# Expert matrices issued in another order, with longer pieces for each partition

## What is computed

```python
grp_logits = (t @ w_r1) + b_r1
grp_prob = jax.nn.softmax(grp_logits, axis=-1)
grp_idx = jnp.argmax(grp_logits, axis=-1)
fine_sel = fine_logits[token, grp_idx]                 # 8 experts of the group
top_val, top_idx = lax.top_k(fine_sel, 2)
gate = grp_gate * jax.nn.softmax(top_val, axis=-1)
exp_idx = grp_idx[:, None] * 8 + top_idx
...
def expert_block(args):
    xb, e = args
    a = jax.nn.silu(xb @ w1[e]) * (xb @ w3[e])         # w1, w3: 1024 x 512
    return a @ w2[e]                                   # w2: 512 x 1024
...
y = y.at[row_tok].add(yb * row_gate[:, None])
```

## Time and profile before

| | us |
|---|---|
| median of 3 runs (lowest, highest) | 3587.39 (3586.43, 3595.63) |
| the profiled execution | 3589.83 |
| its span, first to last instruction | 3588.1 |
| TensorE busy | 3068.5 (86%) |
| VectorE, ScalarE, POOL busy | 1046.3, 747.3, 164.6 |
| DMA traffic | 441.15 MB, of which 201 MB are expert matrices |

### The profile page before, as it was taken

One profiled execution on the slowest core, in us unless ns is written; L12 is line 12 of the kernel. 1 busy time (PEld: TensorE's weight loads), 2 busy tenths in 40 slices (PEclk: granted clock), 3 DMA queues, 4 the chain that ended last, 5 costly groups with the idle time before them and its releaser, 6 DMA issues. The chain is left out here.

```text
span 3588.1 us, 34649 instructions
## 1 busy us (share of the span) xinstructions
PE 3068.5 (86%) x13906; PEld 1847.5 (51%) x13906; DVE 1046.3 (29%) x2162; ACT 747.3 (21%) x1627; POOL 164.6 (5%) x265
## 2 busy tenths in 40 slices
PE   7999974877787588999898999899949774888998
PEld 3448633444444465666455564455523343364674
DVE  3440622000000201055210273333126575200242
ACT  2111810000000102243210383100003110112341
POOL 0000001111110000000000020011100001000000
PEclk9999996899889799999999999999969887999999
DMA  6663432999999311110011200022233414011200
GB/s 228 234 229 124 177 147 62 347 351 365 361 364 358 115 48 32 42 48 24 0 36 60 83 2 1 24 94 87 88 101 132 150 63 148 0 41 53 77 1 24
DMA packets 244208, 441.15 MB, mean 123 GB/s; under 512 B 31420, under 2 KB 111820, under 8 KB 240725
## 3 DMA queue, kind: packets, MB, share of 16 engines
q1 hardware_dynamic: 234278, 416.81, 33.2%
q0 software_dynamic: 9776, 22.18, 1.8%
HBM read 408.73 MB, written 37.81 MB: 124 GB/s over the span
## 5 line engine op out<-in xcount | busy, mean ns | idle before, releaser
L2002 PE MATMUL moe_ph<-expert_weights,moe_x_T 128*64 128x256 f32 x2048 | 275.6, 429 | 100.4 <-issue 99.0
L344 PE MATMUL hyena_in_main<-hT,weight_slots 128*128 128x256 f32 (+1 forms) x1024 | 330.5, 486 | 1.4 <-PEq L985 1.4
L2002 PEld LDWEIGHTS moe_ph<-expert_weights,moe_x_T 128*64 128x64 f32 x2048 | 172.4, 155 | 206.7 <-issue 155.0
L344 PEld LDWEIGHTS hyena_in_main<-hT,weight_slots 128*128 128x128 f32 x1024 | 194.5, 190 | 137.2 <-issue 124.0
L344 PE MATMUL swa_in_main<-hT,weight_slots 128*128 128x512 f32 (+1 forms) x576 | 189.4, 489 | 6.6 <-DMA weight_slots<-b_w_in 5.2
L344 PE MATMUL mla_down_main<-hT,weight_slots 128*128 128x512 f32 (+1 forms) x448 | 168.4, 538 | 19.8 <-DMA weight_slots<-a_w_in 19.8
L1403 PE MATMUL qkv_main<-hT,weight_slots 128*128 128x512 f32 (+1 forms) x384 | 167.8, 580 | 0.9 <-PEq L985 0.9
L1194 PE MATMUL post_y<-expert_weights,hT 128*128 128x512 f32 x384 | 165.1, 592 | 0.0
L344 PEld LDWEIGHTS swa_in_main<-hT,weight_slots 128*128 128x128 f32 x576 | 109.9, 191 | 86.4 <-issue 73.7
L344 PE MATMUL mla_up_main<-expert_weights,weight_slots 128*128 128x512 f32 (+1 forms) x416 | 146.4, 511 | 2.8 <-PEq L985 2.4
L344 PEld LDWEIGHTS mla_down_main<-hT,weight_slots 128*128 128x128 f32 x448 | 88.0, 198 | 100.2 <-issue 75.0
(11 more groups left out here) (357 smaller groups left out, 4117.9 us busy)
## 6 DMA issues: line engine op xcount, KB each, us to landing
expert_weights<-w SPq DMA_DIRECT2D x96, 2048.0 KB, 15.2
first_w_out<-w_mod SPq DMA_DIRECT2D x12, 2048.0 KB
expert_weights<-w_mod SPq DMA_DIRECT2D x12, 2048.0 KB, 8.0
weight_slots<-w_in SPq DMA_DIRECT2D x16, 1024.0 KB
weight_slots<-c_w_in SPq DMA_DIRECT2D x16, 1024.0 KB
weight_slots<-a_w_in SPq DMA_DIRECT2D x14, 1024.0 KB
scr_spectra<-expert_weights SPq DMA_DIRECT2D x12, 1024.0 KB, 3.8
expert_weights<-scr_spectra SPq DMA_DIRECT2D x12, 1024.0 KB, 4.9
```

The lines of the kernel that those rows point to most:

```text
L344: mm = pe.matmul(main[u][0:unit.rows, 0:unit.cols], lhsT, rhs, start=(c == 0), stop=(c == r.kc - 1))
L2002: mm = pe.matmul(bank[half * T:(half + 1) * T, 0:HF], x_T[:, c, :], w[:, c, half * HF:(half + 1) * HF], start=(c == 0), stop=(c == KD - 1))
```

## The change

Two things change.

*Order.* SP's loop now follows the order in which TensorE frees the slots: in step b it waits for the first up product of b and issues W1 of b + 2, waits for the second up product of b and issues W3 of b + 2, then waits for the down product of b - 1 and issues W2 of b + 1. W1 and W3 have a semaphore each, and TensorE waits for W3 only before the second up product.

*Layout.* W1 and W3 are laid out "(p c) n": partition p gets rows 8p to 8p + 7, one contiguous piece of 16 KB. W2 is "(h p j) n": partition p gets rows 2p and 2p + 1 of each half, two pieces of 8 KB. Contraction chunk c now holds the features 8p + c, so the pieces of x that are turned take every 8th column, and the transposes of the activations every 2nd.

```diff
@@ ExpertWeights.__init__
-        self.w1, self.w3, self.w2 = (a[k][0].rearrange("e (c p) n -> e p c n", p=P) for k in ("w1", "w3", "w2"))
+        self.flat1, self.flat3 = flat[0:2], flat[2:4]
+        self.flat2 = [t.rearrange("p (h m) -> p h m", h=2) for t in flat[4:6]]
+        self.w1, self.w3 = (a[k][0].rearrange("e (p c) n -> e p (c n)", p=P) for k in ("w1", "w3"))
+        self.w2 = a["w2"][0].rearrange("e (h p j) n -> e p h (j n)", h=2, p=P)
...
+    def load_gate(self, sp, e):
+
+        sp.dma_start(self.flat1[e % 2], self.w1[e]).then_inc(Stage.w1_in[e % 2], 16)
+
     def load_up(self, sp, e):
 
-        s = e % 2
-        sp.dma_start(self.W1[s], self.w1[e]).then_inc(Stage.w13_in[s], 16)
-        sp.dma_start(self.W3[s], self.w3[e]).then_inc(Stage.w13_in[s], 16)
+        sp.dma_start(self.flat3[e % 2], self.w3[e]).then_inc(Stage.w3_in[e % 2], 16)
 
     def load_down(self, sp, e):
 
-        sp.dma_start(self.W2[e % 2], self.w2[e]).then_inc(Stage.w2_in[e % 2], 16)
+        sp.dma_start(self.flat2[e % 2], self.w2[e]).then_inc(Stage.w2_in[e % 2], 16)
@@ turn_rows
-        mm = pe.matmul(px[:, c * T:(c + 1) * T], x[:, c * P:(c + 1) * P], consts["identity"][0:T, 0:T],
+        mm = pe.matmul(px[:, c * T:(c + 1) * T], x[:, c:D - KD + c + 1:KD], consts["identity"][0:T, 0:T],
@@ turn_act_rows
-        mm = pe.transpose(pa[:, c * P:(c + 1) * P], act_rows[:, c * P:(c + 1) * P], consts["identity"][:])
+        mm = pe.transpose(pa[:, c * P:(c + 1) * P], act_rows[:, c:FF // 2 - 1 + c:2], consts["identity"][:])
@@ experts_stage, SP
-                for b in range(experts.EARLY, E):
-
-                    sp.wait_ge(s_h3, b - 1)
-                    experts.load_up(sp, b)
-                    sp.wait_ge(s_py, b - 1)
-                    experts.load_down(sp, b)
+                for b in range(E):
+
+                    if b + 2 < E:
+                        sp.wait_ge(s_h1, b + 1)
+                        experts.load_gate(sp, b + 2)
+                        sp.wait_ge(s_h3, b + 1)
+                        experts.load_up(sp, b + 2)
+                    if experts.EARLY <= b + 1 < E:
+                        sp.wait_ge(s_py, b)
+                        experts.load_down(sp, b + 1)
@@ experts_stage, TensorE
-                    pe.wait_ge(Stage.w13_in[b % 2], (b // 2 + 1) * 32)
+                    pe.wait_ge(Stage.w1_in[b % 2], (b // 2 + 1) * 16)
                     pe.wait_ge(s_silu, b)
                     up_product(pe, ph1, x_T[b % 2], experts.W1[b % 2]).then_inc(s_h1, 1)
                     if b:
                         turn_act(b - 1)
+                    pe.wait_ge(Stage.w3_in[b % 2], (b // 2 + 1) * 16)
                     pe.wait_ge(s_act, b)
```

More of the change, by code:

```diff
@@ L67 @@
 class Stage:
-    POOLS = ((99, 167), (167, 235))
+    POOLS = ((99, 166), (166, 233))
     turn = 0
@@ L84, in begin @@
         Stage.weights_in = [nc.alloc_semaphore(name=f"weights_in{k}", num=239 + k) for k in range(2)]
-        Stage.w13_in = [nc.alloc_semaphore(name=f"expert_w1_w3_in{k}", num=235 + k) for k in range(2)]
+        Stage.w1_in = [nc.alloc_semaphore(name=f"expert_w1_in{k}", num=233 + k) for k in range(2)]
+        Stage.w3_in = [nc.alloc_semaphore(name=f"expert_w3_in{k}", num=235 + k) for k in range(2)]
         Stage.w2_in = [nc.alloc_semaphore(name=f"expert_w2_in{k}", num=237 + k) for k in range(2)]
@@ L1154, in _ @@
                     for e in range(experts.EARLY):
+                        experts.load_gate(sp, e)
                         experts.load_up(sp, e)
@@ L2252, in step @@
                         sp.wait_ge(s_h3[s], k)
-                        for dst, src in ((W1, experts.w1), (W3, experts.w3)):
-                            sp.dma_start(dst[s], src[ds(e, 1)].rearrange("o p c n -> (o p) c n"))\
+                        for dst, src in ((experts.flat1, experts.w1), (experts.flat3, experts.w3)):
+                            sp.dma_start(dst[s], src[ds(e, 1)].rearrange("o p m -> (o p) m"))\
                                 .then_inc(s_w13[s], 16)
                         sp.wait_ge(s_py[s], k)
-                        sp.dma_start(W2[s], experts.w2[ds(e, 1)].rearrange("o p c n -> (o p) c n")).then_inc(s_w2[s], 16)
+                        sp.dma_start(experts.flat2[s], experts.w2[ds(e, 1)].rearrange("o p h m -> (o p) h m"))\
+                            .then_inc(s_w2[s], 16)
                     over_blocks(sp, step)
```

## The result

The changed kernel takes 3699.3 us (median of 4 runs, 3698.3 to 3700.0), the kernel before in the same comparison 3589.7: a ratio of 1.030, 95% interval 1.028 to 1.032. That is 110 us slower. The forecast was 58 us slower, 3645 us, with a range that ended at 3685; the time lies outside it. The profiled execution has a span of 3698.3 us.

A forecast was written before the change was run, and what follows sets the result against it. The gather loop was to bound every step of the changed kernel: 15.1 + 1.9 (stride) + 2.6 (longer pieces) + 0.6 (clock) = 20.2 us against 18.18, over 29 steps +58 us, 3645 us. Range 3548 to 3685.

The forecast's parts named there:

- The gather loop becomes the bound of all steps: Expert stage: the loop of down product, gather, turning, down product grows from 15.1 to 20.2 us, above the transfers' 15.9.
- The gather among longer pieces, +2.6 us: DMA queues: the gather's small packets take turns with longer weight pieces, so it lands 2.6 us later per step.
- Five and four: Of some 9 weight pieces between an engine's gather and scatter packets, five were taken as 8 KB and four as 16 KB.
- the rival with the engine turning inside a piece: DMA engines switch queues within a piece, so the gather isn't slower: loop 17.0 us, 3553 us; chance 0.22.
- Strided turning, +1.9 us: TensorE's turning of tokens: 16 loads of every 8th column at 235 instead of 116 ns, +1.9 us per expert.
- The rival of a free step of 8: Turning with every 8th column costs nothing extra: loop 17.7 us, -14 us, 3573 us; chance 0.12.
- the prediction's note on lines of 16 bytes: SBUF reads, citing the skill: a step of 8 floats pays, a step of 2 floats does not.
- The clock, +0.6 us: TensorE's clock falls after idling for the gather: between 0 and 2.9 us per step, taken as 0.6.
- First and last step about cancel: Ends of the stage: first loads go out some 4 us earlier, three more turnings on the path cost 5.7.
- The order, up to 0.8 us: SP's load queue no longer runs dry when the down product is late; can return up to 0.8 us per step.
- the 17.4 of the sum from the earlier trace: DMA time per expert in small pieces: W1 and W3 11.4 us, W2 5.3, gather and scatter 0.7.
- Neither cost comes, 15.9 to 16.3 us a step, 3527: Rival: gather not slower and stride free, so transfers bound the stage; -60 us, 3527 us; chance 0.06.

The follow-up runs named there:

- gathers ahead: Changed kernel with POOL issuing each gather four blocks ahead and in front of the scatter: 3542.5 us, ratio 0.986 to the kernel before.
- both comparisons of pieces: Changed kernel with 4 KB pieces (3648.5 us) against the changed kernel; new layout in old order (3709.9) against kernel before with strided turning (3642.7).
- order alone: New order of the loads with the old layout, against the kernel before: 3556.5 us, ratio 0.990.
- gathers ahead in the old layout: Old layout (pieces of 2 and 4 KB) in the new order, with gathers issued four blocks ahead: 3545.2 us, ratio 0.988 to the kernel before.
- gathers ahead and the rows stored in another order: Changed kernel with gathers four blocks ahead and token rows stored so that the turning loads contiguous columns: 3524.5 us, ratio 0.982 to the kernel before.

## Why the prediction was wrong

- **The gather loop becomes the bound of all steps: right.** The issues of W2 lie 20.4 to 23.9 us apart in 28 of 29 steps, where 19.4 and 15.1 alternated, the DMA share is 0.77 (0.8 was named), each turning waits for its gather, and gathers ahead take the loss away.
- **The gather among longer pieces, +2.6 us: right.** 6.7 + 2.6 = 9.3 was the landing expected, 9.3 is the median; both comparisons of pieces give 2.3 and 2.4. How it comes about shows in the queues between 871 and 877 and between 876 and 878, the answer to the earlier trace rows:

```profile
q1 hardware_dynamic: 176, 1.97, 85.9%
q0 software_dynamic: 151, 0.38, 16.6%
...
q1 hardware_dynamic: 55, 0.90, 106.1%
q0 software_dynamic: 33, 0.00, 0.9%
```

  Scatter and gather are 160 packets, as before, and 151 of them go in the 6 us in which the weights' queue moves 176: 112 of 8 KB until 874 and 64 of 16 KB behind it, 7 and 4 for each engine. Five and four had been put in; the 11 pieces of this step make 7 x 0.154 + 4 x 0.463 = 2.9 us by the same prices, so that 2.6 fits so closely is in part luck. In the last 2 us the weights' 55 packets are of 16 KB each and the gather's 33 are tiny, and yet both queues are served. A piece of 16 KB held an engine for 1.061 x 32 / 55 = 617 ns there; 629 had been worked out. (The Trainium skill, "DMA: Bandwidth & Descriptors", SWDGE vs HWDGE vs iDMA, says that the engine goes round robin between its queues and that a packet, the unit of the turns, is preferably 4096 bytes or less. The trace agrees with the turns; the packets here are 16 KB, so the rival with the engine turning inside a piece fell.)
- **Strided turning, +1.9 us: right in size,** 4.0 us against 1.9, +2.1. The rival of a free step of 8 fell. The step of 2 floats is small but not the nothing that the prediction's note on lines of 16 bytes makes of it: the two transposes of the activations take 0.50 us instead of 0.44, their weight loads 207 ns each instead of 142.
- **The clock, +0.6 us: here the prediction failed.** The steps of 21.93 leave 21.93 - 2.8 - 9.3 - 4.0 = 5.8 us for the down product, 2.1 more than the 3.7 of before. The 1.5 us too few make 1.5 x 29 = 44 us, and with 0.2 per step of the turning nearly all of the 52 that were missing. The step of reasoning that failed is "most waits of 1 to 2 us cost nothing, so I take 0.6". It was read off the kernel before, where few turnings wait at all, and "order alone" shows that it does not carry over: with contiguous columns and waits of 1.4 to 2.0 us, 8 down products of 13 took 5.2 us or more. It was not asked what the strided turning does to the clock by itself (5.35 us in 23 of 29 steps, with no wait); nor was a wait of over 4 us priced as the one of 3.00 us in the earlier trace rows, which cost 2.9, though the same paragraph had worked out such a wait for every step. The upper bound of 2.9 was written down and then left out of the range: 15.1 + 1.9 + 2.6 + 2.9 = 22.5 us a step would have given 3712.
- **First and last step about cancel: right** in the sum (+8.5 and -7.0). Of the 8.5 a part is the clock as well: the rows at 633.74.
- **The order, up to 0.8 us: right as a cause, too small.** Alone it gives 18.18 - 16.86 = 1.3 us a step, and the step is then the gather loop's with its clock, not the transfers'. Where short pieces bound the steps, with gathers ahead in the old layout, they are 17.1 us from the sixth on, against the 17.4 of the sum from the earlier trace rows.
- **Neither cost comes, 15.9 to 16.3 us a step, 3527:** not what happened, but the version with gathers ahead and the rows stored in another order comes near the sum of the transfers: 16.2 us a step from the sixth on, against 15.9. That its mean is 15.68 and its time 3524.5, so near the 3527, is in part luck, since its first four steps take 13.0.

## What to carry over

A layout that makes transfers longer has two bills elsewhere: small transfers of another queue wait for whole pieces, and the operand has to be read with a stride by somebody. Look for the loop that carries no large transfer, add both bills to it, and if it becomes the bound take the small transfer out of it (issue it as soon as its buffer is free) and pay the stride once where rows are stored instead of in every product. When two causes can each bring the clock down, removing either shows little or nothing; price such a term at its upper bound, or carry that bound in the range.

## What the runs showed of the hardware

- TensorE's granted clock fell from 2.4 to 1.2 GHz with no idle time at all: behind a turning of 16 strided loads (4.01 us) the down product took 5.35 us instead of 3.65, in 23 of 29 steps. With the same loads among other products the clock was 0.97 and fell in 3 steps of 29, with contiguous loads and the same products behind them it was 0.98. (The Trainium skill, "TensorE: Matmul & The Clock Gate", Part 1: The HAM clock gate, ties the clock to how busy the engine has been of late, and names idling and waits. The falls after a wait agree with that; this one comes without a wait.) Whether it is the slow loads themselves or the products that stand further apart behind them was not separated.
- A wait of 1.4 to 2.0 us for a gather was followed by a down product of 5.2 to 5.35 us in 8 cases of 13 with the new order alone; five waits of 0.9 to 1.6 us in the kernel before by none.
- The strided turning takes 4.0 to 4.1 us whether the clock is at one level or the other, the contiguous one 2.00 us at 2.4 GHz and 3.67 at 1.2 GHz. So at the lower clock a stride costs 0.4 us, not 2.
- The landing of a gather follows the length of the pieces in the other queue: in the median 6.4 to 6.9 us with pieces of 2 and 4 KB (four kernels), 7.0 with 4 KB, 9.3 to 9.5 with 16 and 8 KB; with gathers ahead and 16 KB pieces 8.0 to 8.7.
